# A two-layer block in fp32: modulation products over 2048 columns, one input tile kept in PSUM, and small copies and loads moved to other engines and later places

## The chip, the cores and the metric

The kernel runs on one core of one Trainium2 chip. The metric is device time in microseconds (us) of one execution; less is better. The kernel before takes 3047.72 us, the median of three runs.

In the profile, PE is TensorE (matmul), PEld its weight loads, DVE is VectorE, ACT is ScalarE, POOL is GpSimd, SP is SyncE, whose queue issues the large loads. L1085 is line 1085 of the kernel.

## The reference

The block takes x of 256 tokens by 2048 features and a vector c of 2048, all fp32, through two hybrid layers and then two layers of another kind. The change touches only the hybrid layers:

```python
def hybrid_layer(x, c, positions, w_mod, b_mod, g_pre, g_post, w_in, w_out, ...):
    mod = jax.nn.silu(c) @ w_mod + b_mod              # w_mod [2048, 6144]
    shift, scale, gate = jnp.split(mod, 3, axis=-1)
    h = rms_norm(x, g_pre) * (1.0 + scale[:, None, :]) + shift[:, None, :]
    proj = h @ w_in                                   # w_in [2048, 5648]
    ...                                               # windowed attention, spatial gating,
    ...                                               # gated linear attention; y times silu(z)
    out = y @ w_out                                   # w_out [2048, 2048]
    return x + gate[:, None, :] * rms_norm(out, g_post)
```

The last two layers (attention of three kinds and an MLP of width 8192) are the same in both kernels.

## The kernel before

**Large matmuls.** A list of jobs (`ina0`, `inb0`, `inc0`, `ind0`, `z0`, `out0`, `in1`, ...) is written out ahead, and each job is cut into column tiles and each tile into groups of up to two 128-row chunks of the weights. A group is one step L. Every step loads its weights into one of 10 slots of `raw` (`RAW_SLOTS`; SP's queue, in the order of the list `loads`), ScalarE rounds them into `w_hi` (L785), VectorE subtracts to get the rest `w_lo` (L1085), and TensorE multiplies three times (high by high, low by high, high by low: L1673, L1674, L1675) for both halves of 128 tokens. A slot is free again when TensorE has multiplied its group. ScalarE and VectorE prepare two steps ahead of TensorE (`AHEAD`), at most four (`SPLIT_SLOTS`).

**The input projection of layer 0 comes in four quarters** of the 2048 input features: `ina0`, `inb0`, `inc0`, `ind0`, each 16 steps over 8 tiles of 450 columns. A tile's result in PSUM is copied to `proj` by ScalarE in the first quarter (L810) and added to `proj` by VectorE in the other three (L1109, one operation per token half). The tiles take turns on PSUM banks 0, 1 and 2, 3 (`bank`), so a tile's first matmul waits until the tile two before it has been taken out. Banks 4 and 5 serve the mixers' products that VectorE reads, 6 and 7 the transposes that ScalarE reads.

**Modulation.** `silu(c) @ w_mod` is done by VectorE. The transposed w_mod comes through the same 10 slots, 192 loads of 128 rows by 1024 columns (512 KB) over both layers. `mod_product` multiplies one load by half of the row `c_row`, which lies in all 128 partitions, and sums over the columns (L1128). A slot of this kind is free when VectorE has read it. A table (`pace`) says how many of these loads go before each step: 16 before the first matmul, 16 in each of the first three quarters, 12 in the fourth, 30 in `z0`, 32 in `out0`, 22, 16 and 16 in `in1`, `rest1` and `z1`. A quarter of the input features can be scaled and shifted (`hcol`, L1143, then ScalarE's L861) once its own 16 loads are summed.

**Mixers.** While `z0` (32 steps) runs, the three mixers of the layer are spread between its steps on all engines, in an order written out by hand: rotation of q and k on VectorE (L1237 to L1307), the windowed attention, the spatial gating and the gated linear attention. ScalarE's first work there is a GELU over the columns of u and v (L991). TensorE's first mixer work waits for the rotation.

**Gate rows.** Early in `out0` the gate, a column per 128 features, is turned into rows for all partitions: VectorE makes diagonal matrices (`diagonal`, four operations for each of four, L1550), TensorE multiplies them by a matrix of ones (L1901), and VectorE copies the result into `gp` (L1564). `gp` is used when `out0`'s tiles are taken out.

**The start.** SP's queue loads c to all partitions (1024 KB), the constants (516 KB), the columns and x, then the modulation loads. POOL's queue loads six small tensors (`small_landed`), then writes zeros and loads two rows of weights. VectorE waits for all of these, makes the angle tables, and then begins the products.

```python
            for dst, src in ((cols2[:], io["cols2"]), (stat[:, 32:34].bitcast(I32), io["positions"]),
                             ...
                             (levels[:], io["levels"])):
                pool.dma_start(dst, src).then_inc(S.small_landed, 16)
...
            dve.wait_ge(S.const_landed, 48)
            dve.wait_ge(S.small_landed, 16 * 6)
```

## Time and profile before

| | |
|---|---|
| median of three runs | 3047.72 us (3045.30 to 3049.16) |
| profiled execution: time, span | 3048.0 us, 3046.0 us |
| TensorE busy | 2889.3 us, 95% |
| VectorE busy | 1888.4 us, 62% |
| ScalarE busy | 1475.2 us, 48% |
| mean granted TensorE clock | 0.988 of full speed |
| read from memory | 605.24 MB, 199 GB/s over the span |

The busy shares are means over stages with different limits, so the table says little on an edit in one stage. The page's second part, the span in 40 slices, shows VectorE at six to nine tenths and the DMA engines at five to nine tenths over the first 11 slices (837 us), and VectorE mostly at four to six tenths afterwards, where TensorE is at nine. A window's busy time has to be read against its length, and the granted clock (1.00 is 2.4 GHz, 0.5 is 1.2 GHz) beside it.

### The profile page before, as it was taken

What the parts mean: (1) busy time and instruction counts of PE and PEld (TensorE: products, weight loads), DVE (VectorE), ACT (ScalarE), POOL (GpSimd) and SP (SyncE); (2) the same over time, 40 slices, a digit from 0 to 9 for tenths busy, and PEclk for the clock granted to TensorE, in tenths of its full rate; (3) what the DMA queues carried; (4) which work ended last, traced back from release to release, by engine and by line L of the source; (5) the groups of instructions that cost most, each with busy time, mean ns of one, the idle gap of its engine ahead of it and who ended that gap; (6) DMA issues with size and microseconds to landing.
All of it is one profiled execution on the core that took longest, in us unless ns stands there. A gap on an engine that the chain in (4) does not pass through costs nothing.

```text
span 3046.0 us, 35068 instructions
## 1 busy us (share of the span) xinstructions
PE 2889.3 (95%) x13692; PEld 2429.4 (80%) x13692; DVE 1888.4 (62%) x2432; ACT 1475.2 (48%) x2030; POOL 42.4 (1%) x55
## 2 busy tenths in 40 slices
PE   3998898899998999999999999999999999999998
PEld 3886676788887888788888888888887888888886
DVE  7997998768855547655544555445565555445554
ACT  3436444465545655544434444456546443344443
POOL 0000000000000000000000000000000000000000
PEclk9999998999999999999999999999999999999999
DMA  9996577857665644566556666556445666666663
GB/s 350 329 326 208 183 265 295 297 179 242 223 192 151 174 140 141 159 186 187 190 193 189 187 184 193 184 170 173 139 149 167 187 187 192 193 188 187 200 194 131
DMA packets 297781, 609.66 MB, mean 200 GB/s; under 512 B 19361, under 2 KB 80945, under 8 KB 297105
## 3 DMA queue, kind: packets, MB, share of 16 engines
q1 hardware_dynamic: 295728, 600.74, 62.8%
q0 software_dynamic: 1744, 6.15, 0.7%
q8 instruction: 109, 1.79, 0.2%
q14 instruction: 56, 0.45, 0.1%
q10 hardware_dynamic: 144, 0.52, 0.0%
HBM read 605.24 MB, written 2.10 MB: 199 GB/s over the span
## 4 chain that ended last, share of the span: by engine, by line
PE 76%; DVE 8%; issue 8%; ACT 4%; DMA 3%; POOL 0%; ACTq 0%; DVEq 0%; POOLq 0%; SPq 0%
PE ps L1673 23%; PE ps L1675 23%; PE ps L1674 23%; PE ps L1649 2%; DVE w_lo L1085 2%; DMA raw<-in_w_in 2%; DVE raw L1128 2%; PE ps L1791 1%; PE ps L1777 1%; ACT w_hi L785 1%; PE ps L1685 1%; ACT probs L960 1%; ACT hf L861 1%; DVE proj L1109 1%; ACT hT_hi L866 0%
## 5 line engine op out<-in xcount | busy, mean ns | idle before, releaser
L1085 DVE TENSOR_TENSOR w_lo<-raw,w_hi 128x1024 fp32r<-128x1024 f32 (+4 forms) x988 | 1158.5, 1177 | 1009.5 <-ACT w_hi L785 1006.3
L785 ACT ACTIVATE w_hi<-raw 128x1024 fp32r<-128x1024 f32 (+4 forms) x988 | 1003.8, 1019 | 1232.5 <-PE ps L1675 1067.0
L1673 PE MATMUL ps<-w_hi,hT_hi 128*128 128x512 f32 (+3 forms) x2848 | 1113.3, 391 | 47.3 <-DVE w_lo L1085 16.3
L1675 PE MATMUL ps<-w_hi,hT_lo 128*128 128x512 f32 (+3 forms) x2848 | 1087.4, 382 | 0.0
L1674 PE MATMUL ps<-w_lo,hT_hi 128*128 128x512 f32 (+3 forms) x2848 | 1084.9, 381 | 0.0
L1673 PEld LDWEIGHTS ps<-w_hi,hT_hi 128*128 128x128 f32 x2848 | 540.4, 190 | 145.7 <-issue 25.6
L1675 PEld LDWEIGHTS ps<-w_hi,hT_lo 128*128 128x128 f32 x2848 | 539.2, 189 | 92.3
L1674 PEld LDWEIGHTS ps<-w_lo,hT_hi 128*128 128x128 f32 x2848 | 540.4, 190 | 86.3 <-issue 2.2
L1673 PE MATMUL ps<-w_hi,uT_hi 128*128 128x512 f32 x1024 | 399.7, 390 | 0.1
L1675 PE MATMUL ps<-w_hi,uT_lo 128*128 128x512 f32 x1024 | 398.5, 389 | 0.0
L1674 PE MATMUL ps<-w_lo,uT_hi 128*128 128x512 f32 x1024 | 398.5, 389 | 0.0
L1128 DVE SCALAR_TENSOR_TENSOR raw<-raw,c_row 128x1024 f32<-128x1024 f32 x192 | 232.3, 1221 | 3.7 <-DMA raw<-in_w_modT 2.3
L1673 PEld LDWEIGHTS ps<-w_hi,uT_hi 128*128 128x128 f32 x1024 | 192.2, 188 | 40.7 <-DVE uT_lo L1209 1.2
L1675 PEld LDWEIGHTS ps<-w_hi,uT_lo 128*128 128x128 f32 x1024 | 192.2, 188 | 40.2
L1674 PEld LDWEIGHTS ps<-w_lo,uT_hi 128*128 128x128 f32 x1024 | 192.2, 188 | 39.4
L960 ACT ACTIVATE probs<-probs,smax 128x128 f32<-128x128 f32 (+3 forms) x144 | 65.7, 456 | 96.9 <-DVE smax L1270 94.0
L1649 PE MATMUL ps<-cst,proj 128*128 128x128 f32 x292 | 44.4, 288 | 53.0 <-DVE proj L1529 40.4
L1198 DVE TENSOR_TENSOR hT_lo<-hf,hT_hi 128x512 fp32r<-128x512 f32 x80 | 55.3, 691 | 50.3 <-ACT hT_hi L866 50.1
L1649 PEld LDWEIGHTS ps<-cst,proj 128*128 128x128 f32 x292 | 37.0, 147 | 61.1 <-issue 27.7
L1109 DVE TENSOR_TENSOR x<-x,ps 128x512 f32<-128x512 f32 x80 | 54.7, 684 | 9.9 <-PE ps L1675 8.5
L866 ACT ACTIVATE hT_hi<-hf 128x512 fp32r<-128x512 f32 x80 | 50.5, 632 | 5.7 <-ACT hf L861 0.4
L1649 PEld LDWEIGHTS ps<-cst,probs 128*128 128x128 f32 x216 | 25.7, 140 | 31.6 <-ACT probs L960 23.6
(226 smaller groups left out, 1471.9 us busy)
## 6 DMA issues: line engine op xcount, KB each, us to landing
raw<-in_w_up SPq DMA_DIRECT2D x256, 512.0 KB, 3.7
raw<-in_w_down SPq DMA_DIRECT2D x256, 512.0 KB, 3.7
raw<-in_w_modT SPq DMA_DIRECT2D x192, 512.0 KB, 5.5
raw<-in_w_in SPq DMA_DIRECT2D x128, 456.0 KB, 3.5
raw<-in_w_in SPq DMA_DIRECT2D x88, 512.0 KB, 5.0
raw<-in_w_out SPq DMA_DIRECT2D x64, 512.0 KB, 4.4
raw<-in_w_o SPq DMA_DIRECT2D x64, 512.0 KB, 3.7
raw<-in_w_in SPq DMA_DIRECT2D x64, 450.0 KB, 5.9
```

The source lines that it names most:

```text
L785: act.activation(w_hi[:, L % SPLIT_SLOTS, 0:c, 0:w], raw[:, G % RAW_SLOTS, 0:c, 0:w], ACT.Copy).then_inc(S.hi_ready, 1)
L861: a = act.activation(hf[:, u % 2, c], src[:, c * 2 * P:(c + 1) * 2 * P], ACT.Identity if kw else ACT.Copy, scale=scale[:, k:k + 1], **kw)
L866: act.activation(dst[:, 2 * b:2 * b + 2].rearrange("p c n -> p (c n)"), hf[:, u % 2].rearrange("p c n -> p (c n)"), ACT.Copy).then_inc(S.l ...
L960: a = act.activation(e, e, ACT.Exp, bias=smax[:, r, j:j + 1], accum_out=ssum[:, r, j:j + 1])
L1085: dve.tensor_tensor(w_lo[:, r, 0:c, 0:w], raw[:, r, 0:c, 0:w], w_hi[:, s, 0:c, 0:w].bitcast(F32), ALU.subtract).then_inc(S.group_read, 1)
L1109: a = dve.tensor_tensor(v, v, ps[:, bank(job, i, t), 0:job.width], ALU.add)
L1128: dve.scalar_tensor_tensor(out=w, in0=w, scalar=1.0, in1=c_row[:, part].rearrange("p (c n) -> p c n", n=COLS), op0=ALU.mult, op1=ALU.mult, ...
L1198: dve.tensor_tensor(f(dst_lo[:, 2 * b:2 * b + 2]), f(hf[:, u % 2]), f(dst_hi[:, 2 * b:2 * b + 2]).bitcast(F32), ALU.subtract).then_inc(S.l ...
L1649: mm = pe.transpose(ps[0:rows, b, j * P:(j + 1) * P], s, ident)
L1673: pe.matmul(o, a, wh, start=k0 + c == 0, stop=False)
L1674: pe.matmul(o, a, wl, start=False, stop=False)
L1675: mm = pe.matmul(o, b, wh, start=False, stop=k0 + c == job.chunks - 1)
```

## The change

Six edits, all in the first two layers:

1. **Modulation in pairs.** Two loads of one row block are multiplied by the whole `c_row` in one operation of 2048 columns; where the pair falls on slots 9 and 0, in two operations as before. The pace table counts pairs: 8 before the first matmul, 8, 8, 8 and 4 in the quarters (4 pairs are 8 loads, where there were 12), 17 in `z0` (12 of them in its first 16 steps), 16 in `out0`, then 11, 8 and 8.
2. **A pinned tile.** The eighth tile of the four quarters stays in PSUM banks 4 and 5 and accumulates over all four; ScalarE copies it out once, at the start of the mixers (two operations of 450 columns). The other seven tiles are added by one operation of 2 by 450 columns instead of two of 450. The rotation waits for the first three tiles only.
3. **c in one partition** (8 KB), spread to all partitions by four matmuls with a row of ones; ScalarE's SiLU reads them from PSUM.
4. **Small loads late.** Only `positions` and the first 264 constant columns come at the start; the other constants and the other small tensors are issued by POOL after 8 of the 16 steps of `inc0`. The first writes of zeros to `k1T` and the first reciprocal root on POOL stand ahead of them.
5. **Gate rows.** One VectorE operation per diagonal instead of four, four diagonal buffers instead of two, and the copies to `gp` by ScalarE, through banks 6 and 7.
6. `mod_part` is set to zero at the start, since a pair's sum goes to one of its two columns.

```diff
-for _name, _n in (("ident", 128), ("ones", 128), ("swa", 256), ("chunk", 256), ("tril", 128),
-                  ("inv_freq", HALF), ("cos2", 64), ("sin2", 64)):
+for _name, _n in (("ident", 128), ("ones", 128), ("inv_freq", HALF), ("swa", 256), ("chunk", 256), ("tril", 128),
+                  ("cos2", 64), ("sin2", 64)):
...
+CONST_FIRST = CONST_COLS["swa"][0]
...
+        diag = keys2 + [klev[:, i].rearrange("p k n -> p (k n)") for i in range(2)]
...
-        def mod_group(l, block, part):
-            src = io["w_modT"][l, block * P:(block + 1) * P, part * GROUP:(part + 1) * GROUP]
-            loads.append((src.rearrange("p (c n) -> p c n", n=COLS), 2, COLS))
-            mod_at[l, block, part] = len(loads) - 1
-            return l, block, part, len(loads) - 1
+        def mod_pair(l, block):
+            for part in range(2):
+                src = io["w_modT"][l, block * P:(block + 1) * P, part * GROUP:(part + 1) * GROUP]
+                loads.append((src.rearrange("p (c n) -> p c n", n=COLS), 2, COLS))
+            mod_at[l, block] = len(loads) - 1
+            return l, block, len(loads) - 2
...
-            return [(l, part * KC + q * QC + k, h) for k in range(QC) for part in range(2) for h in range(2)]
+            return [(l, part * KC + q * QC + k) for k in range(QC) for part in range(2)]
...
-            return [(l, 2 * KC + k, h) for k in range(KC) for h in range(2)]
...
-        mods_first = [mod_group(*m) for m in quarter_mods(0, 0)]
+            return [(l, 2 * KC + k) for k in range(KC)]
...
+        mods_first = [mod_pair(*m) for m in quarter_mods(0, 0)]
...
-                    evac="dve" if q else "act"), pace(16, 13) if q < QUARTERS - 1 else pace(12, 16)) for q in range(QUARTERS)]
-        parts += [(Job("z0", w, KC, D, COLS, hT, col0=C_Z), pace(30, 32)),
-                  (Job("out0", io["w_out"][0], KC, D, COLS, hT, evac="dve"), pace(32, 32))]
+                    evac="dve" if q else "act", pinned=True), pace(8, 13) if q < QUARTERS - 1 else pace(4, 16))
+                 for q in range(QUARTERS)]
+        parts += [(Job("z0", w, KC, D, COLS, hT, col0=C_Z), pace(12, 16) + pace(5, 14)),
+                  (Job("out0", io["w_out"][0], KC, D, COLS, hT, evac="dve"), pace(16, 32))]
...
-        parts += [(Job("in1", w, KC, 3 * COLS, COLS, hT, swept=True), [0] + pace(22, 16)),
-                  (Job("rest1", w, KC, rest, rest // 6, hT, col0=3 * COLS), pace(16, 48)),
-                  (Job("z1", w, KC, D, COLS, hT, col0=C_Z), pace(16, 32)),
+        parts += [(Job("in1", w, KC, 3 * COLS, COLS, hT, swept=True), [0] + pace(11, 16)),
+                  (Job("rest1", w, KC, rest, rest // 6, hT, col0=3 * COLS), pace(8, 48)),
+                  (Job("z1", w, KC, D, COLS, hT, col0=C_Z), pace(8, 32)),
...
+        def pinned(job, i):
+            return job.pinned and i == job.turns
...
-            if job.swept and i == 2:
+            if job.swept and i == 2 or pinned(job, i):
...
-            sp.dma_start(c_row[:].rearrange("p c n -> p (c n)"), io["c"][0].partition_broadcast(P)).then_inc(S.const_landed, 16)
-            sp.dma_start(cst[:], io["const"]).then_inc(S.const_landed, 16)
+            sp.dma_start(c_row[0:1].rearrange("p c n -> p (c n)"), io["c"]).then_inc(S.c_landed, 16)
+            sp.dma_start(cst[:, 0:CONST_FIRST], io["const"][:, 0:CONST_FIRST]).then_inc(S.const_landed, 16)
...
-            for dst, src in ((cols2[:], io["cols2"]), (stat[:, 32:34].bitcast(I32), io["positions"]),
+            pool.dma_start(stat[:, 32:34].bitcast(I32), io["positions"]).then_inc(S.positions_landed, 16)
+            pool.memset(k1T[HD:P, :, 0], 0.0).then_inc(S.swa_padded, 1)
+            pool.wait_ge(S.swa_padded, 1)
+            pool.memset(k1T[0:HD, :, 1], 0.0).then_inc(S.swa_padded, 1)
+            pool.wait_ge(S.swa_padded, 2)
+            rsqrt(2)
+            pool.wait_ge(S.group_multiplied, jobs["inc0"].L + 8)
+            for dst, src in ((cst[:, CONST_FIRST:], io["const"][:, CONST_FIRST:]), (cols2[:], io["cols2"]),
...
-                    act.wait_ge(S.dve_evacuated, jobs["ind0"].E + 6)
+                    d = jobs["ind0"]
+                    act.wait_ge(S.group_multiplied, d.L + d.tiles * len(d.groups))
+                    for t in range(TOK):
+                        a = act.activation(proj[:, t, d.turns * d.width:C_Z], ps[:, bank(d, d.turns, t), 0:d.width], ACT.Copy)
+                    a.then_inc(S.pinned_copied, 1)
+                    act.wait_ge(S.dve_evacuated, d.E + 6)
...
-            act.wait_ge(S.const_landed, 48)
-            act.activation(c_row[:], c_row[:], ACT.Silu).then_inc(S.c_ready, 1)
+            act.wait_ge(S.c_spread, 1)
+            act.activation(c_row[:].rearrange("p a n -> p (a n)"), ps[:, 0:4].rearrange("p b n -> p (b n)"), ACT.Silu
+                           ).then_inc(S.c_ready, 1)
+            act.wait_ge(S.const_landed, 32)
...
+                for i in range(D // COLS):
+                    walk.upto(jobs[f"out{l}"].L + 4 + i)
+                    bank_copy(gp[i])
...
-                if job.kind == "inb":
-                    dve.wait_ge(S.act_evacuated, jobs["ina0"].E + i + 1)
+                if job.kind in ("inb", "inc", "ind"):
+                    if job.kind == "inb":
+                        dve.wait_ge(S.act_evacuated, jobs["ina0"].E + i + 1)
+                    v, b = proj[:, :, i * job.width:(i + 1) * job.width], bank(job, i, 0)
+                    dve.tensor_tensor(v, v, ps[:, b:b + TOK, 0:job.width], ALU.add).then_inc(S.dve_evacuated, 1)
+                    return
...
-                    v = (x if job.width == COLS else proj)[:, t, i * job.width:(i + 1) * job.width]
+                    v = x[:, t, i * job.width:(i + 1) * job.width]
...
-            def mod_product(l, block, part, G):
...
-                dve.wait_ge(raw_landed[G % RAW_SLOTS], 16 * (G // RAW_SLOTS + 1))
-                w = raw[:, G % RAW_SLOTS]
-                dve.scalar_tensor_tensor(out=w, in0=w, scalar=1.0, in1=c_row[:, part].rearrange("p (c n) -> p c n", n=COLS),
-                                         op0=ALU.mult, op1=ALU.mult,
-                                         accum_out=mod_part[:, l, block, part:part + 1]).then_inc(S.group_read, 1)
-                if KC <= block < 2 * KC and block % QC == QC - 1 and part:
-                    dve.wait_ge(S.group_read, G + 1)
+            def mod_product(l, block, G):
...
+                for g in (G, G + 1):
+                    dve.wait_ge(raw_landed[g % RAW_SLOTS], 16 * (g // RAW_SLOTS + 1))
+                slot = G % RAW_SLOTS
+                row = c_row[:].rearrange("p a n -> p (a n)")
+                if slot + 1 < RAW_SLOTS:
+                    w = raw[:, slot:slot + 2].rearrange("p s c n -> p (s c n)")
+                    dve.scalar_tensor_tensor(out=w, in0=w, scalar=1.0, in1=row, op0=ALU.mult, op1=ALU.mult,
+                                             accum_out=mod_part[:, l, block, 0:1]).then_inc(S.group_read, 2)
+                else:
+                    for part in range(2):
+                        w = raw[:, (G + part) % RAW_SLOTS].rearrange("p c n -> p (c n)")
+                        dve.scalar_tensor_tensor(out=w, in0=w, scalar=1.0, in1=c_row[:, part], op0=ALU.mult, op1=ALU.mult,
+                                                 accum_out=mod_part[:, l, block, part:part + 1]).then_inc(S.group_read, 1)
+                if KC <= block < 2 * KC and block % QC == QC - 1:
+                    dve.wait_ge(S.group_read, G + 2)
...
-                    dve.wait_ge(S.dve_evacuated, jobs["ind0"].E + 8)
+                    dve.wait_ge(S.dve_evacuated, jobs["ind0"].E + 3)
+                    dve.wait_ge(S.small_landed, 16 * 6)
...
-                    for k in range(4):
-                        a = dve.tensor_scalar(diag[i % 2][:, k * P:(k + 1) * P], ident, gcol[:, 4 * i + k:4 * i + k + 1],
-                                              None, ALU.mult)
-                    a.then_inc(S.diag_ready, 1)
+                    dve.tensor_tensor(diag[i].rearrange("p (k n) -> p k n", k=4), repeat(ident, 4),
+                                      spread(gcol[:, 4 * i:4 * i + 4], P), ALU.mult).then_inc(S.diag_ready, 1)
...
-                dve.wait_ge(S.group_read, mod_at[l, 3 * KC - 1, 1] + 1)
+                dve.wait_ge(S.group_read, mod_at[l, 3 * KC - 1] + 1)
...
-                for i in range(D // COLS):
-                    walk.upto(o.L + 4 + i)
-                    if i + 1 < D // COLS:
-                        diagonal(i + 1)
-                    b = dve_bank()
-                    drained(dve.tensor_copy(gp[i], ps[:, b]))
+                for i in range(1, D // COLS):
+                    walk.upto(o.L + 3 + i)
+                    diagonal(i)
...
-                elif j == 0 and T >= 2:
-                    before = next(b for b in order if b.T <= T - 2 < b.T + b.tiles)
+                elif j == 0 and T >= 2 and not pinned(job, i):
+                    before = next(b for b in order if b.T <= T - 2 < b.T + b.turns)
...
-                        pe.matmul(o, a, wh, start=k0 + c == 0, stop=False)
+                        first, last = k0 + c == 0, k0 + c == job.chunks - 1
+                        if pinned(job, i):
+                            first, last = first and job.kind == "ina", last and job.kind == "ind"
+                        pe.matmul(o, a, wh, start=first, stop=False)
...
-                        mm = pe.matmul(o, b, wh, start=False, stop=k0 + c == job.chunks - 1)
+                        mm = pe.matmul(o, b, wh, start=False, stop=last)
...
+                if l == 0:
+                    pe.wait_ge(S.small_landed, 16 * 6)
+                    pe.wait_ge(S.pinned_copied, 1)
...
-            pe.wait_ge(S.const_landed, 48)
-            pe.wait_ge(S.small_landed, 16 * 6)
+            pe.wait_ge(S.const_landed, 32)
+            pe.wait_ge(S.c_landed, 16)
+            for k in range(4):
+                mm = pe.matmul(ps[:, k], K["ones"][0:1], c_row[0:1, k // 2, k % 2 * COLS:(k % 2 + 1) * COLS],
+                               start=True, stop=True)
+            mm.then_inc(S.c_spread, 1)
...
-                    b = dve_bank()
-                    pe.matmul(ps[:, b], K["ones"], diag[i % 2], start=True, stop=True).then_inc(S.dve_bank_filled, 1)
+                    b = act_bank()
+                    pe.matmul(ps[:, b], K["ones"], diag[i], start=True, stop=True).then_inc(S.act_bank_filled, 1)
```

## Rows read from the trace of the kernel before

**Rows 1.** Windows by stage: stretch, length, busy time of each engine, granted clock, DMA share, GB/s.

```profile
45.50:88.50 43.00, 40.01 (x184) 36.08 (x185) 35.74 (x51) 22.42 (x33) 0.00 (x0) 1.00 0.91 332
88.50:136.50 48.00, 43.01 (x202) 38.14 (x201) 44.41 (x67) 20.58 (x27) 0.00 (x0) 0.96 0.95 337
136.50:185.50 49.00, 42.12 (x201) 36.52 (x200) 45.83 (x70) 18.37 (x22) 0.00 (x0) 1.00 0.92 322
185.50:226.50 41.00, 39.60 (x196) 35.81 (x194) 38.39 (x55) 15.95 (x18) 0.00 (x0) 1.00 0.88 300
239.00:245.40 6.40, 6.01 (x18) 5.08 (x19) 6.12 (x9) 2.14 (x3) 0.00 (x0) 0.50 0.21 83
240.00:316.00 76.00, 69.59 (x351) 55.50 (x350) 54.51 (x100) 45.84 (x103) 0.60 (x1) 0.94 0.54 175
316.00:392.00 76.00, 61.12 (x296) 49.69 (x296) 72.38 (x120) 35.54 (x45) 1.61 (x1) 0.93 0.58 189
420.00:497.00 77.00, 76.96 (x336) 62.39 (x335) 70.11 (x104) 31.12 (x39) 0.00 (x0) 1.00 0.96 342
497.00:591.00 94.00, 73.34 (x312) 58.11 (x312) 73.68 (x105) 44.14 (x61) 4.45 (x6) 0.89 0.78 282
```

**Rows 2.** Timeline of the start: start us, duration us, engine and line, idle before and releaser.

```profile
1.28 0.70 POOL L728 DMA_DIRECT2D cols<-in_cols  x1 [0.45 <-POOL minus_half L721]
...
9.33 1.91 ACT L1014 ACTIVATE c_row<-c_row 128x2048 f32<-128x2048 f32 x1 [7.31 <-DMA cols<-in_cols]
13.67 0.17 DVE L1502 CAST stat<-stat 128x2 f32<-128x2 int32 x1 [13.67 <-DMA levels<-in_levels]
...
18.01 1.23 DVE L1128 SCALAR_TENSOR_TENSOR raw<-raw,c_row 128x1024 f32<-128x1024 f32 x1 [0.30 <-ACT cs L1016]
...
41.34 0.16 DVE L1143 SCALAR_TENSOR_TENSOR hcol<-mod,cols 128x4 f32<-128x4 f32 x1
...
45.49 0.71 PE L1673 MATMUL ps<-w_hi,hT_hi 128*128 128x450 f32 x1 [16.33 <-DVE w_lo L1085]
```

**Rows 3.** DMA issues in the first 60 us: count, size, median us from issue to landing; GB/s per 1.5 us.

```profile
GB/s 0 218 399 354 131 285 426 408 432 399 407 423 423 412 429 415 421 423 412 426 407 421 426 412 405 398 411 400 412 401 407 401 246 0 161 188 208 135 251 400
...
x<-in_x SPq DMA_DIRECT2D x1, 2048.0 KB, 14.4
...
stat<-in_positions POOLq DMA_DIRECT2D x1, 1.0 KB, 5.7
```

**Rows 4.** Timeline of VectorE inside the third quarter.

```profile
139.55 1.28 DVE L1109 TENSOR_TENSOR proj<-proj,ps 128x450 f32<-128x450 f32 x2
140.75 1.22 DVE L1128 SCALAR_TENSOR_TENSOR raw<-raw,c_row 128x1024 f32<-128x1024 f32 x1
...
141.89 1.09 DVE L1085 TENSOR_TENSOR w_lo<-raw,w_hi 128x900 fp32r<-128x900 f32 x1
```

**Rows 5.** Groups of VectorE by shape, 370 to 500 us: busy us, mean ns of one.

```profile
L1151 DVE TENSOR_TENSOR proj<-proj 128x2048 f32<-128x2048 f32 x1 | 2.3, 2287 | 0.0
L1550 DVE TENSOR_SCALAR glx<-cst,gcol 128x128 f32<-128x128 f32 x8 | 1.7, 282 | 0.0
```

**Rows 6.** Waits, 40 to 235 us: who waited for whom, us in total, times, longest.

```profile
ACT w_hi L785 <- DMA raw<-in_w_in: 80.7, 42, 4.3
...
PE ps L1673 <- DVE proj L1109: 11.2, 12, 2.2
```

**Rows 7.** Timeline of TensorE around the start of the mixers.

```profile
230.66 0.50 PE L1673 MATMUL ps<-w_hi,hT_hi 128*128 128x512 f32 x1 [0.95 <-DVE proj L1109]
...
239.38 1.97 PE L1649 MATMUL ps<-cst,proj 128*128 128x128 f32 x8 [2.98 <-DVE glb L1307]
...
241.58 0.63 PE L1674 MATMUL ps<-w_lo,hT_hi 128*128 128x512 f32 x1
```

**Rows 8.** The ones-times-diagonal matmuls: duration ns min/median/max, first and last start.

```profile
L1901 PE MATMUL ps<-glx,cst x8: 590/594/1219, 416.3 to 854.8; 128*128 128x512 f32 x8
```

**Rows 9.** Waits, 505 to 600 us.

```profile
ACT w_hi L785 <- DMA raw<-in_w_in: 32.4, 14, 5.9
```

45 lines of the change are left out of this document (26 added, 19 removed).

## The prediction

> **What bounds the kernel now.** I read the page first: TensorE is busy nearly all of the span, VectorE only in the first third. So a faster VectorE pays only where a window shows it full, and I cut the first third into windows by stage [rows 1]. Compare the busy times with each window's length. In the second and third quarters of the input projection (88.5 to 136.5, 136.5 to 185.5) VectorE is at 44.4 of 48 and 45.8 of 49 us, TensorE at 43.0 and 42.1, the DMA engines at 0.95 and 0.92: VectorE bounds, the DMA engines are next. In the fourth quarter TensorE is at 39.6 of 41. In the attention half of `z0` (240 to 316) TensorE is at 69.6 of 76 and VectorE at 54.5; in its other half (316 to 392) VectorE is at 72.4 of 76. From 420 on, `out0` is TensorE's: 77.0 of 77. In `in1` (497 to 591) no engine is full and the DMA share is 0.78. After `in1`, VectorE's relief should buy nothing.
>
> Then the timeline of the start [rows 2]: VectorE does nothing until 13.67, when the last of POOL's six small loads has landed, makes tables, and begins the products at 18.01. The scaled columns (L1143) are ready at 41.34 and the first large matmul runs at 45.49. The DMA view [rows 3] shows 400 to 430 GB/s from 9 to 48 us without a gap.
>
> **The start: -5.3 us.** POOL's first load is issued at 1.28 [rows 2]; `positions` takes its place, and landed 5.7 us after its issue [rows 3], so about 7.0. The tables take 18.01 - 13.67 = 4.3, to 11.3. Beside them, c goes another way. `cols1` had landed by 9.33 [rows 2], behind 1.54 MB that are now 0.14; I take 5. The four spreading matmuls have the shape of L1901, at most 1.22 us each at the slow clock [rows 8]: 9.9. SiLU over the same 2048 columns took 1.91 [rows 2]: 11.8. Third, the bytes: x (2.1 MB), two modulation loads (1.05 MB) and 0.2 MB of small ones, at 415 GB/s 8.1 us, from about 2.2, with some 1.5 for landing: 11.8. All three meet at 12, six earlier than 18.01. From there to 41.34 there were 16 products at 1.14 (below), 18.2, and 5.1 of normalizing and sums. Now 8 pairs at 2.21 take 17.7, but the first three wait for their loads, 1.05 MB at 415 GB/s = 2.53 a pair, +0.6. The columns come some 6 us earlier. I take -5.3, since the POOL landing is one sample; bounds -3 (landing at 9.5) and -6.5.
>
> **A pair against two products.** The spacing of products is 141.89 - 140.75 = 1.14 [rows 4]. 1024 columns at the rate between the two rows below are 1.07, so 0.07 is what an operation costs beyond its columns. The nearest row for 2048 columns is y times silu(z), 2.29 long [rows 5]; a 1024-column operation is 1.22 long and spaced 1.14, so the long one should be spaced 2.21. A pair saves 0.07 us: 0.6 a quarter, 6.7 over 96 pairs if VectorE were always on the path; bounds 0 (one in ten pairs falls on slots 9 and 0 and is not joined) and 0.16.
>
> By the Trainium skill (VectorE: DVE Perf Modes, "The TRN2 errata") an fp32 operation takes (N + 151)/0.96 ns, and a large tile pays the fixed part once. By that a pair saves 0.157 us, 15 over 96, and this sum would be about 2 us lower. The durations here agree (1.22 and 2.29), but successive starts are only 0.07 beyond the columns, so the page's fixed part mostly overlaps the next operation.
>
> **The quarters: -4.3 us.** An evacuation of one tile holds VectorE 140.75 - 139.55 = 1.20 [rows 4]; 900 columns in one operation, as `w_lo` has them, 1.01 to 1.09. Seven instead of eight: 9.6 - 7.6 = 2.0 a quarter, in three quarters. With the pairs, VectorE loses 2.6 of the 47 to 48 us of the second and third quarters. TensorE waited 11.2 us for L1109 [rows 6], which is this. The DMA floor is just below: 16 loads of 524 KB and 16 of 461 KB are 15.8 MB, 38 us at 415 GB/s. But a pair waits for its second load and frees the first slot a product later, and 1.4 MB of late small loads (3.4 us of DMA time) fall in the third and fourth quarters. So -2.0 for the second and -1.5 for the third, bounds 0 and -2.6 each. The first quarter has no evacuation on VectorE (35.7 of 43): -0.5. The fourth is TensorE's: -0.3; its four loads fewer only free VectorE and DMA.
>
> **Into the mixers: -4.9 us.** `z0`'s first tile waited 0.95 us for an evacuation [rows 7]; with seven turns, the tile whose bank it takes is out earlier: -1.0. TensorE waited 2.98 us for the rotation, and its next matmuls ran at the slow clock (granted 0.5 from 239 to 245.4 [rows 1], the lower of its two levels, 1.2 GHz, so some 3.2 us more than at 2.4). VectorE comes to the rotation one evacuation (1.2) earlier and no longer behind the last tiles, but with a pair (2.21) where one product stood: I take -2.2 for the wait and half of the slow stretch, -1.7. Bounds: 0 and -7.2. The pinned tile's copies (by the SiLU's 1.91 for 2048 columns, two of about 0.5) stand on ScalarE before the GELU and what follows it, the rounding of `z0`'s fifth group; ScalarE then waits for TensorE only, which is past. Without that cover they cost 1.0.
>
> **The attention half of `z0`: +3 us.** Up to 24 loads' products stand there instead of 15: 12 x 2.21 - 15 x 1.14 = 9.4 us more on VectorE, which idles 21.5 of 76 [rows 1]. In three steps of four a pair stands where a product was, 1.07 later for the softmax behind it; the chain scores, maximum, exponent, transposes goes through VectorE once a step. Its idle time is some 1.4 a step over 15 steps, but not all in front of the softmax; I let 0.4 of each 1.07 through, 12 x 0.4 = 5, less what the free fourth step gives back: +3; bounds 0 and +9.
>
> **The other half, into `out0`: -5.8 us.** Up to the gate's diagonals, 19 products fall to 7 pairs: 21.7 - 15.5 = 6.2 us less where VectorE is at 95%. I take -5.5, bounds -2 and -6.2. The first diagonal is one operation instead of four (0.28 long each [rows 5]): -0.3. The other diagonals and the `gp` copies then lie beside TensorE, which is full, so nothing; on ScalarE (31 of 77 busy) the copies have room. `out0` has no slack in DMA (0.96): a loss there is in the rivals.
>
> **`in1`: +1 us.** ScalarE waits 32.4 us for loads there [rows 9]: slots come back late, and 11 pairs each keep one slot a product (1.1) longer. Bounds 0 and +12.
>
> **The rest: 0.** In `rest1`, `z1` and `out1` TensorE is full. The POOL memsets and reciprocal root run earlier, POOL being idle; its late loads are used after the input projection. Only the gating's rows are now behind them, needed 150 us later.
>
> **Sum.** -5.3 - 4.3 - 4.9 + 3 - 5.8 + 1 = -16.3. On the profiled execution (3048.0, of which 3046.0 the span) 3031.7; it stands 0.3 above the median, so 3031.5. I say 3032.
>
> **Rivals.**
> (a) *The DMA engines bound the quarters, and pairs wait for slots.* For it: a share of 0.92 to 0.95 [rows 1], 80.7 us of ScalarE waiting for loads [rows 6]. Against: VectorE is busy through most of those waits. The quarters give 0 instead of -4.3, `in1` loses 4 instead of 1: 3039. The Trainium skill (DMA: Bandwidth & Descriptors, "Specifications") puts a core's memory limit at 358 GB/s: 15.8 MB would take 44 us, still under 48, so the saving would be as forecast, without more. The trace does not agree with that limit: 400 to 430 GB/s hold for 39 us [rows 3].
> (b) *The attention half pays in full*, +9 for +3, because the softmax stands behind every pair, and the slow clock at the mixers' start stays (+1.7): 3040.
> (c) *More is gained*: the extra products hide in VectorE's idle time (0), the rotation wait and its slow clock go away whole (-7.2 for -4.9), the start gives -6.3: 3025.
> (d) *Slower: the pairs starve the slots.* A slot held 1.1 us longer delays a load, then `w_hi`, `w_lo` and a matmul. 24 pairs in three quarters and 11 in `in1` could put 35 x 1.1 = 39 us on the path. The gains are gone when some two fifths of it land there; with 60%, 23 us, the quarters giving nothing: 3055. Against it: loads and products come in one order, and ten slots hold 13 us of DMA work, ten times the delay.
>
> **Chances.** Forecast 0.50 (3027 to 3036), (a) 0.20, (b) 0.12, (c) 0.13, (d) 0.05. A measurement of this kernel can tell about 0.2%, 6.1 us. Faster by more than that, under 3041.6: all of the forecast and (c), nearly all of (a) and (b): 0.86. Within: 0.10. Slower: 0.04. The range takes in (a), (b) and most of (c): 3023 to 3043.
>
> **What the profile after would show.** First product at about 12 us and first large matmul near 40. Products of 2048 columns spaced 2.2; evacuations of about 1.09. The second and third quarters at 46 and 47.5 us with TensorE's wait for L1109's successor mostly gone; if they stay at 48 and 49 with VectorE idle behind loads, (a). A wait for the rotation under 1 us. 240 to 316 longer by a few us, with TensorE waiting for probabilities; 316 to 415 shorter by 5 to 6. The prediction is wrong if the spreading matmuls or `positions` come late, or if VectorE's waits for modulation loads add up to tens of us.

## The result, and the profile after

The changed kernel takes **3057.14 us** (median of 6 runs, 3054.25 to 3062.69); the kernel before, on the same chip, 3046.97 (3045.30 to 3049.16). The ratio is 1.0035, 95% interval 1.0022 to 1.0048: slower by 7 to 15 us, where I had forecast 15 faster. The profiled execution took 3054.25, its span 3052.2, 6.2 longer than that of before. Of the variants below, two hold one execution far slower than the rest (b2 4178 us, its profiled one, so that no trace of it is used; f3 6518 us), which counts in their medians but not in their ratios.

I cut the trace at each job's first large matmul. Stretch and length, busy time of TensorE, its weight loads, VectorE, ScalarE and POOL, granted clock, DMA share, GB/s, for `ina0`, `inb0`, `inc0`, `ind0`, `z0`, `out0`, `in1`, `rest1`, `z1`:

```profile
40.90:87.70 46.80, 43.26 (x201) 39.06 (x202) 38.12 (x40) 23.96 (x36) 0.00 (x0) 1.00 0.85 307
87.70:135.40 47.70, 42.71 (x202) 38.02 (x201) 42.96 (x46) 19.97 (x26) 0.00 (x0) 0.96 0.93 336
135.40:189.20 53.80, 43.32 (x202) 38.56 (x201) 43.56 (x45) 17.86 (x23) 4.33 (x8) 0.94 0.90 322
189.20:228.20 39.00, 39.00 (x193) 36.22 (x192) 34.75 (x36) 16.09 (x17) 0.00 (x0) 1.00 0.84 288
228.20:405.00 176.80, 149.12 (x731) 120.00 (x730) 149.94 (x239) 93.31 (x159) 4.70 (x3) 0.92 0.61 204
405.00:517.80 112.80, 95.46 (x411) 75.49 (x409) 96.53 (x114) 52.66 (x72) 4.46 (x6) 0.94 0.85 307
517.80:600.50 82.70, 72.97 (x312) 58.19 (x313) 59.36 (x60) 37.38 (x50) 0.00 (x0) 0.96 0.80 284
600.50:733.40 132.90, 124.37 (x793) 117.64 (x793) 89.81 (x155) 77.41 (x152) 1.84 (x2) 0.99 0.62 194
733.40:844.70 111.30, 106.84 (x516) 88.57 (x515) 97.45 (x127) 59.92 (x71) 2.55 (x1) 0.98 0.68 230
```

Cut the same way, the jobs before are 46.5, 48.9, 49.1, 40.7, 172.2, 115.3, 79.0, 131.2 and 109.6 long. (The windows of [rows 1] are not this cut: `z0`'s first matmul is at 230.66 [rows 7], not at 226.5, and the second and third quarters run from 92.0 to 190.0, so each of those windows opens one to two steps before its quarter. The busy times change little: VectorE 44.6 of 48.9 and 46.0 of 49.1.) The start gained 4.6, the second quarter 1.2, the third lost 4.7, the fourth gained 1.7 (four loads fewer stand in it), `z0` lost 4.6, `out0` gained 2.5, `in1` lost 3.7, `rest1` and `z1` together 3.4. What the reader should see is VectorE in the third row: 43.6 busy of 53.8, where it had 46.0 of 49.1. It was relieved as intended, and the quarter got longer: TensorE was busy for 43.3 of it, with the granted clock at 0.94, and idle for 10.5.

The start went nearly as forecast. Its timeline (start, duration, engine and line, idle before and releaser):

```profile
3.86 0.17 DVE L1546 CAST stat<-stat 128x2 f32<-128x2 int32 x1 [2.80 <-DMA stat<-in_positions]
...
10.84 1.88 ACT L1039 ACTIVATE c_row<-ps 128x2048 f32<-128x2048 f32 x1 [8.82 <-PE ps L1940]
...
12.93 2.29 DVE L1166 SCALAR_TENSOR_TENSOR raw<-raw,c_row 128x2048 f32<-128x2048 f32 x1 [5.03 <-ACT cs L1043]
```

The first product starts at 12.93 for 18.01 [rows 2]. From 85 to 187 us, nearly all of the second and third quarters, the waits are these (who waited for whom, us in total, times, longest):

```profile
ACT w_hi L805 <- DMA raw<-in_w_in: 59.7, 23, 6.8
PEld ps L1715 <- DVE proj L1139: 18.5, 8, 7.5
PE ps L1715 <- DVE proj L1139: 15.5, 8, 7.2
DVE w_lo L1115 <- ACT w_hi L805: 10.0, 13, 2.7
...
DVE raw L1166 <- DMA raw<-in_w_modT: 2.5, 3, 1.5
```

TensorE still waits for the evacuation, 15.5 us where [rows 6] had 11.2 (40 to 235 us; over that stretch it is 15.5 here too), though VectorE has less to do. The longest of these waits, on ScalarE, VectorE and TensorE:

```profile
168.30 0.95 ACT L805 ACTIVATE w_hi<-raw 128x900 fp32r<-128x900 f32 x1 [6.79 <-DMA raw<-in_w_in]
```

```profile
166.51 0.08 DVE L1166 DVE_READ_ACCUMULATOR raw<-raw,c_row 128x1 f32 x1
169.28 1.10 DVE L1115 TENSOR_TENSOR w_lo<-raw,w_hi 128x900 fp32r<-128x900 f32 x1 [2.69 <-ACT w_hi L805]
170.30 1.08 DVE L1139 TENSOR_TENSOR proj<-proj,ps 128x900 f32<-128x900 f32 x1
```

```profile
171.44 0.74 PE L1715 MATMUL ps<-w_hi,hT_hi 128*128 128x450 f32 x1 [7.18 <-DVE proj L1139]
```

Read it backward. TensorE waits 7.18 us for a PSUM bank. The operation that frees it takes 1.08 and needs only matmuls that are long done. It is late because VectorE takes its operations in the order of the program, and ahead of it stands a `lo` for a group that TensorE needs *later* than the bank. That `lo` waits 2.69 for ScalarE, which waited 6.79 for a load. VectorE is idle meanwhile, which no sum of busy times shows. The two waits that I had put down to VectorE's being full, TensorE's for L1109 [rows 6] and ScalarE's for loads, were one.

### The profile page after: what moved, and what is told of

Read it like the earlier page. It is cut to its first block, busy times and chain, and to the rows that moved or that the text cites. A ratio compares the mean times of both kernels' runs of the same rounds, so it can differ in the third digit from the quotient of the medians.

```text
span 3052.2 us, 34953 instructions
## 1 busy us (share of the span) xinstructions
PE 2896.8 (95%) x13700; PEld 2434.2 (80%) x13700; DVE 1870.1 (61%) x2210; ACT 1479.4 (48%) x2038; POOL 43.8 (1%) x56
## 4 chain that ended last, share of the span: by engine, by line
PE 72%; issue 7%; DVE 4%; ACT 3%; DMA 1%; POOL 0%; DVEq 0%; POOLq 0%; ACTq 0%
PE ps L1715 22%; PE ps L1717 22%; PE ps L1716 22%; PE ps L1688 2%; PE ps L1819 1%; PE ps L1833 1%; DVE w_lo L1115 1%; PE ps L1727 1%; DMA raw<-in_w_in 1%; ACT w_hi L805 1%; DVE raw L1166 1%; ACT hf L881 1%; DMA raw<-in_w_modT 0%; ACT probs L980 0%; ACT hT_hi L886 0%
## 5 line engine op out<-in xcount | busy, mean ns | idle before, releaser
L1716 PEld LDWEIGHTS ps<-w_lo,hT_hi 128*128 128x128 f32 x2848 | 540.8, 190 | 87.1 <-issue 1.9
L1166 DVE SCALAR_TENSOR_TENSOR raw<-raw,c_row 128x2048 f32<-128x2048 f32 x82 | 187.2, 2287 | 21.2 <-DMA raw<-in_w_modT 14.8
L980 ACT ACTIVATE probs<-probs,smax 128x128 f32<-128x128 f32 (+3 forms) x144 | 65.7, 456 | 97.9 <-DVE smax L1312 95.0
```

What stands on the lines that cost most here:

```text
L980: a = act.activation(e, e, ACT.Exp, bias=smax[:, r, j:j + 1], accum_out=ssum[:, r, j:j + 1])
L1166: dve.scalar_tensor_tensor(out=w, in0=w, scalar=1.0, in1=row, op0=ALU.mult, op1=ALU.mult, accum_out=mod_part[:, l, block, 0:1]).then_inc(S ...
L1716: pe.matmul(o, a, wl, start=False, stop=False)
```

## The experiments

All are variants of the changed kernel unless said otherwise. Medians are in us; ratios are to the kernel before, measured on the same chip beside each. Differences between variants are taken from the ratios, times 3047. Lengths of stages come from one profiled run each, and a stage with the same code varies between runs: the second and third quarters together take 101.5, 98.0 and 99.1 us in the changed kernel, f1 and f3, which are the same there, and 96.3 and 102.7 in c1 and c2, whose pairs are two operations. So a stage is compared by several runs or by its gaps. `rest1` and `z1` together vary little: 244.1 to 244.4 in the changed kernel, b3, c1, c2 and e1.

**The pairs and their places.** b1 takes the fused products back to single ones, b2 keeps the pairs with the old pacing, b4 does both, b3 moves the late small loads.

```diff
 b1, b4: mod_product(l, block, part, G): wait for load G; one operation over 1024 columns; group_read + 1
 b2 (pairs):
-  "ind0" pace(4, 16); "z0" pace(12, 16) + pace(5, 14)
+  "ind0" pace(6, 16); "z0" pace(15, 32)
 b3:
-  pool.wait_ge(S.group_multiplied, jobs["inc0"].L + 8)
+  pool.wait_ge(S.group_multiplied, jobs["ind0"].L + 4)
```

> Theory P (pairs hold slots: the first load's slot stays taken until the second load has landed and both are multiplied, so later loads start late): the changed kernel with products of 1024 columns again, the same number of loads at each place, gives back in1 (96.2 to about 91.5 us), rest1 and z1 (3.4 us together) and the first quarter (1.6), so 3046 to 3048 where the changed kernel has 3057. Theory L (the late small loads cost, in the third quarter) expects the third quarter still about 54 us long and a total of 3055 or more. Theory Z (the new distribution over ind0 and z0) expects no change either.

> Pairs kept, but 6 pairs in the fourth quarter and 15 spread evenly over z0, the amounts of before. Theory Z expects z0 about 3 us shorter and 3053 to 3054; theories P and L expect no change beyond 2 us, since in1, rest1, z1 and the third quarter are as they were; the fourth quarter may be a few us longer.

> The late small loads issued after 4 of the 16 steps of the fourth quarter instead of 8 of the third. Theory L: the third and fourth quarters together 3 to 5 us shorter, TensorE's 7 us wait for an evacuation in the third quarter gone, total 3052 to 3054. Theory P alone: no change, 3057.

> Products of 1024 columns and the old amounts, the rest of the change kept (pinned tile, start, late loads, gate rows). Theory P with the start's gain of 4.6: 3043 to 3046. If it stays at 3055 or more, neither pairs nor amounts are the cause. Against b1 it tells what the new amounts do by themselves: theory Z says this one is 3 us faster, my prediction said 2 to 3 us slower.

| | median | lowest to highest | ratio, interval |
|---|---|---|---|
| b1 | 3042.50 | 3037.42 to 3044.15 | 0.9985, 0.9975 to 0.9994 |
| b2 | 3063.30 | from 3056.99 | 1.0052, 1.0036 to 1.0069 |
| b3 | 3052.72 | 3051.19 to 3057.31 | 1.0028, 1.0016 to 1.0039 |
| b4 | 3039.66 | 3036.67 to 3046.58 | 0.9981, 0.9970 to 0.9991 |

The pairs are the loss: 15 us between the changed kernel and b1, 22 between b2 and b4. The pacing is not: the old one makes no difference with single products (b1, b4), and with pairs it is no better (b2, 5 slower, the intervals overlapping). Moving the small loads out of the third quarter gives some 2, which the intervals do not separate from nothing; but TensorE's longest wait in that quarter falls from 7.18 to 2.59 us and the quarter from 53.8 to 48.3, while the two jobs behind it get 1.6 and 2.4 longer.

**Is it the fusion?** c1 does a pair as two operations, each with its own wait and release, at the same place; c2 does two operations but waits for both loads first. c1 undoes all that rival (d) was made of, the slot held longer, and c2 the part of it that comes after the second load has landed.

```diff
-                dve.scalar_tensor_tensor(out=w, in0=w, scalar=1.0, in1=row, ...).then_inc(S.group_read, 2)
 ...
+                for part in range(2):                        # c1; in c2 both waits stand ahead of the loop
+                    dve.wait_ge(raw_landed[(G + part) % RAW_SLOTS], 16 * ((G + part) // RAW_SLOTS + 1))
+                    ...
+                    dve.scalar_tensor_tensor(out=w, in0=w, scalar=1.0, in1=c_row[:, part], ...).then_inc(S.group_read, 1)
```

> The changed kernel with the loads still listed in pairs, but each pair as two products of 1024 columns; each waits for its own load and frees its own slot. Theory P (waiting for the second load and holding the first slot): most of the 14 us that the single products gave back, so 3043 to 3047, and rest1 and z1 together about 239.5 us instead of 244.0. Theory B (bunching: two products stand in one place and what is queued behind them on VectorE comes 2.2 us late in one step and not at all in the next): no recovery, 3054 to 3058, rest1 and z1 at 243 to 245.

> As the one before, but both loads are waited for ahead of the first product; each product still frees its own slot. If waiting for the second load is the cost: as the changed kernel, 3055 to 3058, with the two products in their own waits at 3043 to 3047. If holding the first slot until the end is the cost: 3043 to 3047 here too. Theory B: 3054 to 3058 in both.

c1: 3059.71 (3055.53 to 3060.66), 1.0050 (1.0033 to 1.0067). c2: 3057.99 (3056.65 to 3059.10), 1.0043 (1.0028 to 1.0058). Neither gives anything back. So it is neither the fused operation nor its slots that cost. What is left is that two products stand behind each other in every second step, instead of one in each, or that their two loads do: c1 and c2 keep both, and f1 below tells the two apart in `rest1` and `z1`. What joining saves, at most the 6.7 us that I had, these measurements can't tell: c1 and c2 are 5 and 2 us slower than the changed kernel, with overlapping intervals.

**Is VectorE or the DMA the bound of the quarters?** From b4. d1 multiplies 512 of each product's 1024 columns and leaves the others out; d2 loads 512 of 1024 columns and multiplies them twice, so that its sums are over half of the weights.

```diff
 d1:
-                w = raw[:, G % RAW_SLOTS]
+                w = raw[:, G % RAW_SLOTS, 0]                 # in1=c_row[:, part, 0:COLS]
 d2:
-            loads.append((src.rearrange("p (c n) -> p c n", n=COLS), 2, COLS))
+            loads.append((src.rearrange("p (c n) -> p c n", n=COLS), 1, COLS))
 ...                                                          # src with COLS columns; two products over the same COLS
```

> From the kernel with single products and the old amounts (3039.7): each product takes only the first 512 columns of its load, the second half is left out; the loads stay whole. VectorE has 0.53 us less per product, 8.5 us per quarter. If VectorE bounds the quarters (my prediction), the second and third quarter go from 46 and 50 us to 41 or 42 (TensorE's time), 3 to 9 us each, total 3020 or less. If the DMA engines and their slots bound them, the quarters stay within 2 us and only the linear-attention half of z0 gains: total 3030 to 3036.

> From the same kernel: each modulation load brings only 512 of its 1024 columns, and VectorE multiplies them twice (2 x 512 columns, 1.2 us, where one product took 1.14); the other 512 are left out. Half of the modulation's DMA time is gone with VectorE as busy as before. If the DMA engines bound the quarters: the second and third come to 43 to 45 us, in1 to 80 to 85, total 3015 to 3025. If VectorE bounds them: quarters and total unchanged but for in1, 3032 to 3040.

d1: 3023.52 (3020.89 to 3029.04), 0.9932 (0.9916 to 0.9948). d2: 3031.24 (3030.19 to 3034.11), 0.9957 (0.9942 to 0.9972). Their second and third quarters, d1 first (b4's take 99.1 us, with VectorE busy for 87.1 and a DMA share of 0.96):

```profile
81.40:182.00 100.60, 84.87 (x401) 76.02 (x400) 71.18 (x120) 37.83 (x47) 4.33 (x8) 0.95 0.94 328
```

```profile
84.40:180.60 96.20, 84.34 (x401) 74.66 (x401) 88.10 (x152) 37.49 (x46) 4.33 (x8) 0.98 0.81 257
```

In d1 VectorE is busy 71 of 101 us, and the quarters are no shorter: TensorE waits 15.7 us for the evacuation, in b4 14.5. In d2 the DMA share falls to 0.81, and the quarters are 2.9 us shorter than b4's, within the spread of that stage. Neither is the bound there. The gains of both lie mostly elsewhere: d1 reaches the first large matmul 3.6 us earlier (36.8 for 40.4) and gains 12.5 in `z0` and `out0`; d2 gains 3.5 in the first quarter, 4.0 in `z0` and 3.9 in `in1`.

**Is it the order?** `evacuate` goes ahead of the step's product and `lo`, in the quarters alone. e1 has that with pairs, e2 with single products (from b4), f2 in the kernel before, with nothing else. e4 is e2 with b3's place of the small loads. e3 is b4 without the tile that stays in PSUM: all eight tiles are evacuated by VectorE in each quarter, each in two operations of 450 columns, and the rotation waits for all of them, as before.

```diff
                 for job, i, j, L, splits in ahead(order):
+                    if prev and j and job.kind in ("inb", "inc", "ind"):
+                        evacuate(*prev)
+                        prev = None
                     for m in mods_at.get(L, ()):
                         mod_product(*m)
```

> The changed kernel, but in the second to fourth quarters VectorE adds the tile before into proj (L1139) ahead of the step's modulation product and of the group's lo, instead of behind them. Theory O (order: TensorE waits for an evacuation that stands behind a product pair and a lo, whose rounding waits for a late load): TensorE's idle time in the second and third quarters (4.99 and 10.48 us in the changed kernel) falls to under 4 together, the two quarters from 101.5 to about 94 us, and the kernel to some 3048 us. Rival D (the loads themselves are late, whatever stands before the evacuation): TensorE waits as long, now for the lo of its group instead of for the evacuation; the two quarters stay within 2 us of 101.5 and the time at 3055 to 3059.

> The version with products of 1024 columns and the old pacing (median 3039.7), with the evacuation ahead of product and lo as in the run before. Theory O: the two quarters fall from 96.1 to about 91 to 92 us, the kernel to some 3035. Rival D: 96 us as before, 3039 to 3040. If the order were all that made pairs costly, this kernel and the one with pairs would come out alike; I expect pairs to stay 10 us dearer, since most of their loss (about 9 of 14 us) lies after the quarters.

> Products of 1024 columns, old pacing, and no tile kept in PSUM: all eight are evacuated in each quarter, each in two operations of 450 columns as before. What is left of the change is the start, the late small loads, the gate rows on ScalarE and the diagonals in one operation. Theory L (VectorE has idle time in the quarters, so a tile's evacuation less is worth little): the quarters 47 to 48 and 50 us, z0 about 173, the kernel within 2 us of 3039.7. Rival V (my prediction: an evacuation less takes 2 us off a quarter, and the mixers' start gains some 3): 6 to 9 us slower, 3046 to 3049.

> The second of these runs, and the late small loads issued four steps into the fourth quarter instead of eight steps into the third. If 1.4 MB of small loads in the third quarter are what makes its loads late (one stretch of slow clock, 6.8 us long, stands there), the third quarter falls by 3 to 4 us and the fourth rises by 1 to 2: some 2 us faster than the second run. If the order of the evacuation already hides them: the same time within 1 us.

> The kernel before the change, with the evacuation of the quarters ahead of the step's product and lo, and nothing else. If the order on VectorE's queue is what TensorE waits for in the second and third quarters, and not VectorE's being full (44.4 of 48 and 45.8 of 49 us busy), both quarters shrink without any work being taken from VectorE: from 96.3 to 91 to 93 us, and the kernel to 3040 to 3042. If VectorE's fullness were the bound: 96 us and 3046.

| | median | lowest to highest | ratio, interval | 2nd and 3rd quarter |
|---|---|---|---|---|
| e1 | 3048.91 | 3046.33 to 3050.90 | 1.0005, 0.9996 to 1.0014 | 93.4 |
| e2 | 3032.91 | 3030.25 to 3034.96 | 0.9949, 0.9936 to 0.9963 | 90.7 |
| e3 | 3045.74 | 3041.45 to 3051.12 | 0.9996, 0.9988 to 1.0005 | 104.1 |
| e4 | 3029.91 | 3028.23 to 3033.01 | 0.9943, 0.9930 to 0.9955 | 86.6 |
| f2 | 3038.56 | 3035.52 to 3041.07 | 0.9967, 0.9956 to 0.9979 | 91.4 |

(The two quarters take 97.9 us before, 101.5 in the changed kernel and 99.1 in b4.) The order alone gives 9 us with pairs (e1 against the changed kernel), 10 with single products (e2 against b4), 10 in the kernel before (f2), with no work taken from any engine. f2's two quarters, then its fourth:

```profile
92.10:183.60 91.50, 82.77 (x401) 73.84 (x402) 89.50 (x136) 38.06 (x47) 0.00 (x0) 1.00 0.96 349
183.60:222.60 39.00, 39.00 (x193) 36.23 (x192) 38.58 (x57) 15.91 (x17) 0.00 (x0) 1.00 0.90 314
```

Of the 6.5 us that the two quarters lose, some 4 are TensorE's idle time and some 2 its clock: the same matmuls keep it busy for 82.8 us at a granted clock of 1.00, where before they took 85.0 at 0.97 and 1.00. The fourth quarter has no idle time of TensorE left, 39.0 us for 40.7. In the second and third TensorE still waits 8.7 us for the evacuation, where it had 10.3 before, and VectorE is now at 89.5 of 91.5: *here* it may be the bound, but its work was not halved in this kernel. With a tile's evacuation less, the order takes more of these waits away: from 15.5 to 6.0 us with pairs (e1, and 2.4 for `lo`), from 14.5 to 6.3 with single products (e2). e4's second and third quarter, and its waits:

```profile
85.40:171.90 86.50, 82.48 (x401) 73.65 (x400) 85.91 (x120) 37.33 (x46) 0.00 (x0) 1.00 0.99 368
```

```profile
ACT w_hi L804 <- DMA raw<-in_w_in: 44.1, 24, 5.7
...
PE ps L1709 <- DVE proj L1138: 2.9, 4, 1.3
```

ScalarE still waits 44 us for loads (52 in b4), and TensorE 2.9 for the evacuation (14.5 in b4): a late load now costs little, since what TensorE needs first no longer stands behind it. The DMA share is 0.99 and VectorE at 85.9 of 86.5. The Trainium skill (DMA: Bandwidth & Descriptors, "Specifications") puts a core's memory limit at 358 GB/s; e4 moved 368 over 86.5 us, so this trace, with one core at work, does not agree with that limit. e3 is 4.6 to 6.1 us slower than b4 (by the ratios, by the medians): the tile that stays in PSUM, with its joined evacuations, does pay, some 5 us.

**Where the pairs lose the rest.** e1 is still 17 us slower than e2, so most of the loss lies after the quarters. The clearest gaps are in `rest1` and `z1`. In the changed kernel, VectorE, ScalarE, and TensorE before one of them:

```profile
626.83 2.28 DVE L1166 SCALAR_TENSOR_TENSOR raw<-raw,c_row 128x2048 f32<-128x2048 f32 x1
629.04 0.08 DVE L1166 DVE_READ_ACCUMULATOR raw<-raw,c_row 128x1 f32 x1
629.04 0.87 DVE L1115 TENSOR_TENSOR w_lo<-raw,w_hi 128x688 fp32r<-128x688 f32 x1
629.83 0.16 DVE L1305 COPY probs<-sinks 128x4 f32<-128x4 f32 x1
629.90 0.68 DVE L1307 SCALAR_TENSOR_TENSOR probs<-ps,cst 128x512 f32<-128x512 f32 x1
630.61 0.69 DVE L1312 TENSOR_REDUCE smax<-probs 128x4 f32<-128x516 f32 x1
```

```profile
631.34 0.40 ACT L980 ACTIVATE probs<-probs,smax 128x129 f32<-128x129 f32 x1 [3.37 <-DVE smax L1312]
```

```profile
633.47 0.48 PE L1688 MATMUL ps<-cst,probs 128*128 128x128 f32 x1 [2.43 <-ACT probs L980]
```

The softmax stands behind the pair, which holds VectorE for 2.21 us; in b4 it stands behind one product, and the same gap is 1.37. f1 takes the products away there (the 16 pairs of `rest1` and `z1` multiply 16 of 2048 columns, the rest is left out; the loads stay), and f3 lists these pairs three and two steps earlier in their period.

```diff
 f1:
+                if l == 1 and (block >= 2 * KC):
+                    w = raw[:, slot, 0, 0:16]                # in1=c_row[:, 0, 0:16], group_read + 2
 f3:
-  "rest1" pace(8, 48); "z1" pace(8, 32)
+  "rest1" pace(8, 48)[3:] + pace(8, 48)[:3]; "z1" pace(8, 32)[2:] + pace(8, 32)[:2]
```

> The changed kernel, with the 16 pairs of rest1 and z1 multiplied over 16 of their 2048 columns only; their loads are issued and waited for as before, and the rest of these products is left out. Theory S (a pair stands on VectorE ahead of the softmax or the chain step that TensorE waits for): TensorE's gaps of 2.43, 2.05 and 1.61 us before the transposes of probabilities and the level products shrink by about 1.1 to 2.2 each, rest1 and z1 together from 243.99 to 239 us or less, and the time to some 3051. Rival D (the loads of the pairs, which come two in a row, are what is late): gaps and time as in the changed kernel.

> The changed kernel with its pairs of rest1 and z1 listed three and two steps earlier in their period. Theory S: which of TensorE's waits for VectorE's chain are long changes, since a pair now stands in front of other parts of it; rest1 and z1 together come out between 238 and 247 us instead of 243.99. If the pairs cost the same wherever they stand, the gaps stay at 2.43, 2.05 and 1.61 and the time at 3057.

TensorE's gaps at three places, and the two jobs together:

| | softmax of `rest1` | a later one | levels in `z1` | `rest1` + `z1` | ratio, interval |
|---|---|---|---|---|---|
| b4 | 1.37 | 0.90 | 0.43 | 239.1 | 0.9981, 0.9970 to 0.9991 |
| changed | 2.43 | 2.05 | 1.61 | 244.2 | 1.0035, 1.0022 to 1.0048 |
| f1 | 0.33 | under 0.3 | under 0.3 | 236.2 | 1.0001, 0.9991 to 1.0011 |
| f3 | under 0.3 | under 0.3 | under 0.3 | 238.6 | 1.0009, 0.9999 to 1.0018 |

f1's median is 3049.35, f3's 3050.50. One product more in front costs 1.06, 1.15 and 1.18 a place, and the gaps go with the products, while the loads are as they were, still two in a row. So in `rest1` and `z1` it is the products that cost, not the order of their loads. Moved to another step, the same 16 pairs open none of the three gaps, and one of 0.87 elsewhere in `rest1`. f3's waits in the two jobs, where the changed kernel has 5.2 (3) and 2.1 (3, longest 1.6) for the same two lines:

```profile
PE ps L1688 <- ACT probs L980: 2.4, 4, 0.9
...
PE ps L1886 <- DVE klev L1420: 0.5, 2, 0.2
```

**All mends together.** g1 has the pairs with e1's order, b3's small loads and f3's places; g2 is e4 with its single products of `rest1` and `z1` one step earlier.

```diff
 g2:
-  "rest1" pace(16, 48); "z1" pace(16, 32)
+  "rest1" pace(16, 48)[1:] + [0]; "z1" pace(16, 32)[1:] + [0]
```

> The changed kernel with its pairs kept and three places mended: evacuation first in the quarters, the late small loads four steps into the fourth quarter, and the pairs of rest1 and z1 moved three and two steps. If the mends add (8 us from the first, some 3 from the second, 5 from the third), about 3041 to 3043 us: still some 10 above the version with single products, since the pairs in z0 and in1 stay as they are. If they don't add: 3046 or more.

> The fastest version so far (single products, evacuation first, small loads in the fourth quarter; 3029.9) with the products of rest1 and z1 one step earlier. Its gaps there are smaller (1.37, 0.90 and 0.43 us), so if it is only a matter of what stands behind a product, 1 to 3 us can be had: 3027 to 3029. If the place matters for pairs only: 3030.

g1: 3040.07 (3036.39 to 3046.61), 0.9984 (0.9973 to 0.9996). The mends, 9, 2 and 8 us by their ratios, add up to 19; g1 is 16 below the changed kernel: about additive. g2: 3030.61 (3028.49 to 3035.80), 0.9957 (0.9941 to 0.9972): no gain over e4. The fastest is **e4, 3029.91, ratio 0.9943**: the change without its pairs, with the evacuation first and the small loads in the fourth quarter.

## Why the prediction was wrong

The terms of the forecast beside the profiles, by the cuts above (the measured column adds up, but for rounding, to the 6.7 us by which `z1` ends later; a stretch at the lower clock is counted at half its length):

| | forecast | measured |
|---|---|---|
| start | -5.3 | -4.6 |
| four quarters | -4.3 | +3.1 |
| into the mixers | -4.9 | -2.0 |
| attention half of `z0` | +3 | +4.0 |
| the other half, into `out0` | -5.8 | -0.8 |
| `in1` | +1 | +3.7 |
| `rest1`, `z1` | 0 | +3.4 |

- **The start, -5.3:** right, 5.1 earlier at the first product and 4.6 at the first large matmul (40.9 for 45.49). `positions` landed after 2.5 us (forecast 5.7), and the tables were not what the product waited for. The spreading matmuls began at 3.6 instead of 5, but took 7.2 us instead of 4.9: each of the four stands in the trace as two matmuls, 0.85 apart, as each of the eight of L1901 does (16 there, of which [rows 8] shows the half that reads `glx`). SiLU so began at 10.84, forecast 9.9. The 1.5 us that I had for landing in the sum of the bytes stood on no row; here loads of 132 and 90 KB landed 2.2 and 2.0 us after their issue, and the product did not wait for them. The other kernels with this start reach the first large matmul at 40.3 to 42.2 (d1, with half of each product, at 36.8).
- **The quarters, -4.3: the step that failed first.** I wrote "VectorE bounds, the DMA engines are next", from 44.4 of 48 and 45.8 of 49 us. Busy shares of 0.93 do not make a bound when TensorE, VectorE, ScalarE and a load wait for each other in a loop. d1 and d2 show that neither VectorE's time nor the bytes set these quarters once the tile is pinned (100.6 and 96.2 us for b4's 99.1), e1, e2 and f2 that the order sets 8.1, 8.4 and 6.5 us of them with VectorE's work as it was. What I read as VectorE's fullness was in good part the `lo` in front of the evacuation; how much was left of it in the kernel before is open, since f2 has VectorE at 98%.
- **The pinned tile** was worth some 5 us (e3 against b4), 5.0 in the second and third quarters of the profiles (99.1 for 104.1), where I had 2.0 a quarter: about the right size, and given away again by the late small loads. e3, with the new start but all eight evacuations, has 104.1 in these quarters where before has 97.9: I had counted 3.4 us of DMA time for the small loads as 0.5 in the third quarter and nothing behind it. In the changed kernel POOL issues them from 157.9 to 161.7, and the loads behind them are the latest of the quarter (the wait of 6.79 us above ends at 168.3); moved, they give 2 us (b3, e4).
- **A pair against two products, -0.07 each:** there in the rows (2.21 from the start of a pair to the next operation, 2.29 for the two products of c2), too small to be seen in the times (c1, c2).
- **Into the mixers, -4.9:** the 0.95 us in front of `z0`'s first tile are gone, as forecast (they count in the fourth quarter's 1.7). The wait for the rotation was 3.41 us for 2.98 [rows 7], not 0.8, with two products in front of it. The stretch at the lower clock behind it was 3.4 us (granted 0.52) for 6.1 (0.50), which saves some 1.4 where I had 1.7.
- **The attention half of `z0`, +3:** from the rotation to the last late softmax 73.1 us for 70.5, +2.6, and that with the shorter slow stretch in it; without that some +4. Near enough, with 10 pairs' worth of products for 13 single ones in place of the 12 for 15 that I had.
- **The other half, -5.5: wrong place.** I took 19 products falling to 7 pairs off the stretch up to the gate's diagonals. Up to the chain's last gap (76.7 us for 76.5) there are 13 products and then 6 pairs: 1.6 us less on VectorE, and nothing gained. That a pair in front of the levels costs as in `z1` fits, but was not tried by itself: the longest gap grew from 5.5 to 6.5, and one before the spatial mixer, the cause of which is not settled, from 3.0 to 6.0. The relief behind it, up to the first gate matmul, where the products had been dense, gave 1.8 (28.2 us for 30.0).
- **`in1`, +1:** 3.7. Over all kernels here, those with pairs have 82.7 to 86.5 there, those without 79.0 to 82.0 (d1 and d2 aside). Rival (d) had put it down to slots; c1 frees the first slot early and has 85.3, so the slot is excluded; that it is the place of the products here too fits the waits, but was not tried by itself: they stand in front of the `hT_lo` that TensorE waits for (11.5 us for 7.4 between 505 and 600).
- **The rest, 0: the other step that failed.** `rest1` and `z1` cost 3.4 beside before, 5.1 beside b4. "TensorE is full" was true of the averages, 124.4 of 132.9 and 106.8 of 111.3; the gaps that a product can widen are what is left. I had priced the pair in front of the softmax in `z0` and put it at nothing here; f1 and f3 show it.

The rival on the slower side (d) named a result that came, near its 3055, by a mechanism that did not: the slots were not starved. Its own terms, 23 us on the forecast and nothing from the quarters, would make 3059. Rival (a), the DMA engines and slots, falls with d2 and c1. The one that I did not list is bunching, the same work at half the places and twice the length.

What stays open: which of the pairs in `z0` cost how much (with pairs `z0` and `out0` together take 289 to 296 us, without 282 to 288, d1 and d2 aside), whether there and in `in1` it is the products or their loads that should not stand two in a row, and why the gap before the spatial mixer grew.

## What to carry to other kernels

On an in-order queue, ask of each operation what stands *behind* it: what frees a bank or a slot goes ahead of what waits for a load. Moving one such operation gave 10 us here with no work saved, more than the 5 of taking an eighth of the evacuations away. And two short background operations in one place, joined or not, are dearer than one in each of two places where a latency chain crosses the same queue; if they must stand together, choose the step. A share of 0.93 on two engines at once can be the sign of a loop and not of a bound: halve the suspect's work and look before building on it.

## What the runs showed of the hardware

- Two VectorE products of 1024 columns behind each other hold the engine for 2.29 us (c2), one of 2048 for 2.21 (the changed kernel): 0.08 saved. By the Trainium skill (VectorE: DVE Perf Modes, "The TRN2 errata") the saving should be 0.157 us, by my estimate from it 15 over 96 pairs if all of them lay on the path; the rows show half of it a pair, and c1 and c2, 5 and 2 us above the changed kernel by their ratios with overlapping intervals, do not show 15.
- A tiny load on POOL's queue landed 2.5 us after its issue with 8 and 132 KB issued ahead of it, and 5.7 with 1024 and 516 KB ahead [rows 3].
